# Cross attention's key and query units as products of 512 columns, with VectorE adding the halves

## What is computed

```python
def memory_attention(h, mem_n, w_q, w_kv, w_out):      # h: 256 x 1024, mem_n: 256 x 1024
    q = (h @ w_q).reshape(b, s, XA_HEADS, XA_HEAD_DIM)  # 4 heads of 256
    k, v = jnp.split(mem_n @ w_kv, 2, axis=-1)
    sc = jnp.einsum('bshd,bmhd->bhsm', q, k) * XA_HEAD_DIM ** -0.5
    p = jax.nn.softmax(sc, axis=-1)
    o = jnp.einsum('bhsm,bmhd->bshd', p, v).reshape(b, s, D_MODEL)
    return o @ w_out
```

## Time and profile before

| | |
|---|---|
| median of 3 runs | 1280.35 us (1280.28 to 1281.39) |
| the profiled execution | 1280.76 us, of which the trace's span is 1278.9 us |
| TensorE matmul busy | 1252.3 us, 98% of the span |
| VectorE, ScalarE, GpSimd busy | 929.4 us (73%), 680.6 us (53%), 77.9 us (6%) |
| mean granted TensorE clock | 0.998 of full speed |

### The profile page before, as it was taken

How to read it: one execution, slowest core, us unless ns; L and a number is a source line. 1 busy time by engine, 2 the same in 40 slices (tenths; PEclk the granted TensorE clock), 3 DMA queues, 4 the chain that set the end, 5 groups by cost and what they waited for, 6 DMA issues and landing times. The chain is left out here.

```text
span 1278.9 us, 18653 instructions
## 1 busy us (share of the span) xinstructions
PE 1252.3 (98%) x7688; PEld 1115.2 (87%) x7688; DVE 929.4 (73%) x1290; ACT 680.6 (53%) x868; POOL 77.9 (6%) x94
## 2 busy tenths in 40 slices
PE   7999999999999999999999999999999999999997
PEld 7878999989988888889998888888888988988886
DVE  5665857775456666575997997788888858788877
ACT  5555253443553444454776655466655564566652
POOL 2010000101000000000002331000000000000000
PEclk9999999999999999999999999999999999999999
DMA  8664555656535665546556654565554643655550
GB/s 284 209 184 132 166 164 166 219 192 199 180 99 164 197 187 182 192 137 197 177 185 205 202 189 149 198 198 195 181 186 134 204 154 108 213 183 188 198 194 37
DMA packets 159748, 227.98 MB, mean 178 GB/s; under 512 B 5517, under 2 KB 122001, under 8 KB 159536
## 3 DMA queue, kind: packets, MB, share of 16 engines
q1 hardware_dynamic: 156544, 216.68, 53.1%
q0 software_dynamic: 2816, 9.52, 2.3%
q10 hardware_dynamic: 304, 0.59, 0.1%
HBM read 225.68 MB, written 1.10 MB: 177 GB/s over the span
## 5 line engine op out<-in xcount | busy, mean ns | idle before, releaser
L1244 DVE TENSOR_TENSOR wlo<-raw,whi 128x2048 fp32r<-128x2048 f32 (+3 forms) x188 | 419.7, 2244 | 118.9 <-ACT whi L789 118.5
L789 ACT ACTIVATE whi<-raw 128x2048 fp32r<-128x2048 f32 (+2 forms) x187 | 348.0, 1874 | 19.8 <-DMA raw<-in_w_xkv 6.6
L2045 PE MATMUL psum<-h_both,whi 128*128 128x512 f32 x714 | 254.7, 396 | 0.0
L2013 PE MATMUL psum<-h_both,whi 128*128 128x256 f32 x704 | 200.6, 285 | 0.2 <-DVE wlo L1244 0.2
L2044 PE MATMUL psum<-h_both,wlo 128*128 128x256 f32 x714 | 199.4, 279 | 0.3 <-DVE h_both L1289 0.3
L2015 PE MATMUL psum<-h_both,wlo 128*128 128x256 f32 x704 | 199.1, 283 | 0.0
L2014 PE MATMUL psum<-h_both,whi 128*128 128x256 f32 x704 | 199.1, 283 | 0.0
L2013 PE MATMUL psum<-whi,r_hi 128*128 128x512 f32 (+1 forms) x464 | 181.0, 390 | 1.4 <-DVE arena L1588 0.7
L2015 PE MATMUL psum<-whi,r_lo 128*128 128x512 f32 (+1 forms) x464 | 178.1, 384 | 0.0
L2014 PE MATMUL psum<-wlo,r_hi 128*128 128x512 f32 (+1 forms) x464 | 178.0, 384 | 0.0
L2045 PEld LDWEIGHTS psum<-h_both,whi 128*128 128x128 f32 x714 | 134.0, 188 | 27.6
(11 more groups left out here) (331 smaller groups left out, 1858.2 us busy)
## 6 DMA issues: line engine op xcount, KB each, us to landing
raw<-in_ffn_up SPq DMA_DIRECT2D x44, 1024.0 KB, 5.1
raw<-in_w_in SPq DMA_DIRECT2D x32, 1024.0 KB, 5.8
raw<-in_ssd_in_proj SPq DMA_DIRECT2D x24, 1024.0 KB, 5.4
raw<-in_ffn_down SPq DMA_DIRECT2D x22, 1024.0 KB, 4.9
raw<-in_w_up SPq DMA_DIRECT2D x16, 1024.0 KB, 5.5
raw<-in_w_down SPq DMA_DIRECT2D x16, 1024.0 KB, 4.9
raw<-in_w_xkv SPq DMA_DIRECT2D x8, 1024.0 KB, 5.4
raw<-in_ssd_out_proj SPq DMA_DIRECT2D x8, 1024.0 KB, 5.0
```

Of the source, the lines that this page charges most:

```text
L789: A(whi[u % SLOTS][:, 0:kt * n], raw[u % SLOTS][:, 0:kt * n], ACT.Copy).then_inc(hi_split, 1)
L1244: V.tensor_tensor(wlo[s][:, 0:kt * n], raw[s][:, 0:kt * n], whi[s][:, 0:kt * n].bitcast(F32), ALU.subtract).then_inc(lo_split, 1)
L2013: M(o, a_hi, b_hi, start=start, stop=False)
L2045: return M(b[:, :], w_hi_k, h_both[:, :, k, :], start=False, stop=k == kt - 1)
```

## The change

Key and query units are made by `both_unit` instead of `b_unit`. Each gets two banks, 0 and 1 or 2 and 3 in turn. `r_hi` and `r_lo` become halves of one tensor `r_both`, so that the query's activations can be one moving operand. On ScalarE `copy_bank` becomes `low_copy`, and on VectorE `add_halves` is put in: for key unit j ahead of the j-th of the four splits behind `rms_out`, for query unit k at the end of head step k, behind the low part of a head's output. "Drained" of these keys is now signalled by VectorE.

```diff
     for j in range(4):
         p.unit(("xk", j), w["w_xkv"][0], 0, KD, 256 * j, 256)
-        p.gemm(("xk", j), ("xk", j))
+        for c in range(2):
+            p.gemm(("xk", j, c), ("xk", j), 2 * (j % 2) + c)
...
             p.unit(("xq", k), w["w_xq"][0], 0, KD, 256 * k, 256)
-            p.gemm(("xq", k), ("xq", k))
+            for c in range(2):
+                p.gemm(("xq", k, c), ("xq", k), 2 * (k % 2) + c)
...
-        r_hi, r_lo = sb("r_hi", [P, KD, T], F32R), sb("r_lo", [P, KD, T], F32R)
+        r_both = sb("r_both", [P, 2, KD, T], F32R)
+        r_hi, r_lo = r_both[:, 0], r_both[:, 1]
...
                 hi()
-                copy_bank(kT[:, 2 * j:2 * j + 2, :], ("xk", j), pair)
+                low_copy(kT[:, 2 * j:2 * j + 2, :], [("xk", j, c) for c in range(2)])
...
                     hi()
-                    copy_bank(qT[:, 2 * k:2 * k + 2, :], ("xq", k), pair)
+                    low_copy(qT[:, 2 * k:2 * k + 2, :], [("xq", k, c) for c in range(2)])
...
             rms_out(hN, xn, 0, 2)
-            for _ in range(4):
+            for j in range(4):
+                add_halves(kT[:, 2 * j:2 * j + 2, :], 0, [("xk", j, c) for c in range(2)])
                 lo()
...
                 if k >= 3:
                     part_bank(h_lo, h_hi, ("xo", k - 3), slice(2 * (k - 3), 2 * (k - 3) + 2))
+                if k < XA_HEADS:
+                    add_halves(qT[:, 2 * k:2 * k + 2, :], 0, [("xq", k, c) for c in range(2)])
                 if k >= XA_HEADS:
                     lo()
...
             for j in range(4):
-                b_unit(at[("xk", j)], h_hi, h_lo, one(("xk", j)))
+                both_unit(at[("xk", j)], [("xk", j, c) for c in range(2)])
...
                 if k < XA_HEADS:
-                    b_unit(at[("xq", k)], r_hi, r_lo, one(("xq", k)), ready=None if k else xT_ready("h2"))
+                    both_unit(at[("xq", k)], [("xq", k, c) for c in range(2)], x_both=r_both, ready=None if k else xT_ready("h2"))
                 if 1 <= k <= XA_HEADS:
                     i = k - 1
-                    wait_drained(pe, ("xk", i))
-                    wait_drained(pe, ("xq", i))
+                    for c in range(2):
+                        wait_drained(pe, ("xk", i, c))
+                        wait_drained(pe, ("xq", i, c))
```

More of the change, by code:

```diff
@@ L813, in copy_bank, with low_copy @@
                 A(dst, src(b), ACT.Copy).then_inc(drained[use[key][0]], 1)
+            def low_copy(dst, keys):
+                b0 = use[keys[0]][0]
+                for key in keys:
+                    wait_bank(act, key)
+                A(dst, psum[:, b0:b0 + 2, T:2 * T], ACT.Copy).then_inc(low_out, 1)
             def xT_parts(name, dst):
@@ L956, in _ @@
                 scaled_part_bank(h_hi[:, 2 * j:2 * j + 2, :], ("h3", j), G_MLP + 2 * j)
[L958 to L963, removed]
             def mlp_group(g):
@@ L2037, in b_unit, with both, both_unit @@
                 last.then_inc(unit_used, 1)
-            def both(b, w_hi_k, w_lo_k, k, kt):
+            def both(b, w_hi_k, w_lo_k, k, kt, x_both=h_both):
                 if k == 0:
[L2042 to L2047, removed]
+                    M(b[:, :], w_hi_k, x_both[:, :, k, :], start=True, stop=False)
+                    return M(b[:, 0:T], w_lo_k, x_both[:, 0, k, :], start=False, stop=False)
+                M(b[:, 0:T], w_lo_k, x_both[:, 0, k, :], start=False, stop=False)
+                return M(b[:, :], w_hi_k, x_both[:, :, k, :], start=False, stop=k == kt - 1)
+            def both_unit(u, keys, between=None, x_both=h_both, ready=None):
                 w_hi, w_lo, kt, _ = weights(u)
@@ L2054, in both_unit @@
                     for k in range(kt):
+                        if ready is not None and c == 0:
+                            ready(k)
                         cs = slice(P * c, P * c + P)
-                        last = both(b, w_hi[:, k, cs], w_lo[:, k, cs], k, kt)
+                        last = both(b, w_hi[:, k, cs], w_lo[:, k, cs], k, kt, x_both)
                 last.then_inc(unit_used, 1)
```

## The result

The changed kernel took 1288.02 us (median of 4 runs, 1287.65 to 1288.62), against 1280.32 for the kernel before beside it (4 runs): a ratio of 1.0055 [1.0043, 1.0068]. That is 7.7 us slower, where +3.77 was forecast and 1285.8 was the end of the range. The direction was right, the size was off by twice.

What follows compares the result with a forecast made beforehand. TensorE, busy 1252.3 of 1278.9 us, was taken to bound the kernel. The terms -1.36 + 2.45 + 0.05 + 2.63 = +3.77 us on a median of 1280.35 gave 1284.1 us, range 1282.6 to 1285.8.

Steps and rivals of the forecast that it cites:

- Part 1: All eight key and query units: wider products take 5.59 us a unit instead of 5.76, -1.36 us in all.
- Place A: Key unit 2 waits for the sums of key unit 0, behind VectorE's split and hN: +2.45 us.
- Place B: The value units wait for the sums of key unit 2: +0.05 us, ends 0 and 0.3.
- Place C: Scores 3 wait for the sums of query unit 3, behind head 0's low part on VectorE: +2.63 us.
- rival 4: Key and query units: wider products win little, units stay near 5.7 us; +4.8, 1285.1 us; chance 3%.
- Part 2: Evacuation: ScalarE's copy stays, VectorE gains 5.9 us of additions; three places can wait, elsewhere the additions are hidden.
- handoff: At the new waits: TensorE goes on 0.05 us after VectorE's addition ends.
- restart: After a wait, the first product holds the next back by 0.34 instead of 0.23 us.
- Rival 1: Only one of the two large waits binds: +1.1, 1281.5 us, within 0.2%; chance 8%.
- Rival 2: Time lost at the waits is made up at later TensorE waits: +0.3, 1280.6 us; chance 5%.
- rival 3: The clock falls to 1.2 GHz at the waits for one unit, 5.6 us each: 1289.7 or 1295.3 us; chance 4%.

Runs made afterwards that it cites:

- e12: The changed kernel measured once more, unedited: 1287.02 us, ratio 1.0042; its profiled execution is the run of 1285.23 us.
- e6: The kernel before, with one added wait: key unit 2 starts only when hN is written; 1283.36 us, ratio 1.0016.
- e1: The changed kernel with its query units put back as before, so only the key units are changed; 1284.18 us, ratio 1.0024.
- e3: The changed kernel with each query unit's sums moved ahead of the maximum of the scores in VectorE's order; 1284.52 us, ratio 1.0023.
- e2: The changed kernel with its key units put back as before, so only the query units are changed; 1283.88 us, ratio 1.0021.
- e7: The changed kernel with key unit 0's sums put between the two tiles of hN, shortening the wait at key unit 2; 1286.21 us, ratio 1.0035.
- e4: The changed kernel with key units 2 and 3 in banks 4 to 7; 1283.02 us, ratio 1.0015.
- e9: The changed kernel with nine unread matmuls of 512 columns into a free bank ahead of key unit 2; 1287.75 us, ratio 1.0051.
- e8: The kernel before, with one added wait: key unit 2 starts only when VectorE has split the first value unit; 1288.19 us, ratio 1.0056.
- e5: The changed kernel with the edits of both e3 and e4; 1279.71 us, ratio 0.9992.
- e10: The kernel before, with eight unread matmuls ahead of the transpose behind the second block's norm; 1280.33 us, ratio 0.9992.
- e11: e5 with eight unread matmuls ahead of the transpose behind the second block's norm; 1279.90 us, ratio 0.9991.

## Why the prediction was wrong in size

Against the execution without a fall (e12), step by step, shifts read as in the first section:

| step | forecast | measured |
|---|---|---|
| Part 1, eight units | -1.36 | -1.28 (5.59 us a unit in after; 0.16 each) |
| Place A, key unit 2 | +2.45 | +2.64 (-0.36 to +1.80 with three units at -0.16) |
| Place B, value units | +0.05 | +0.17 (value unit at 314.32 in after, 5.75 behind unit 3's start) |
| Place C, scores 3 | +2.63 | +2.83 (+1.20 to +4.03) |
| nothing | 0 | -0.36 at the start, +0.3 behind 367 us |
| sum | +3.77 | +4.3, inside the ends of +3.1 and +4.9 |

**Part 1** was right, and with it rival 4 was wrong: the rows of the MLP unit held for key and query units. **Part 2** was right: 16 additions more, VectorE 6.1 us busier (5.9 forecast), ScalarE's time unchanged, and no wait where the additions were called hidden. **Places A and C** were right in place and releaser, and each was 0.2 us too small. The term that was short is the handoff from VectorE's end to TensorE's start, which the prediction took from one pair of rows as 0.05 us and used for both: it measured 0.15 at key unit 2 and 0.25 to 0.28 at scores 3. (At key unit 2 the additions also began 13.14 us behind unit 0's start, where 13.07 was laid out.) The restart was right (301.32 to 301.63 in e12 is 0.31 us, against 0.23 in a stream). That the trace shows 2.35 and 2.56 us of idle time where 2.35 and 2.53 were forecast is luck: it counts from the modelled end of the last matmul, the forecast from the moment at which the next one could have started. Counted like the forecast the waits are 2.52 and 2.72. **Place B** was within its ends. **Rival 1** fell with both waits in every profile of the change. **Rival 2** fell with e6, where a shift of +1.95 us behind the wait was still +1.96 at 804 us.

**The step that failed: the sum has no term for the clock.** The prediction left it to rival 3, with 4% and the wrong size, because the longest pause inside the kernel, 2.2 us, had not moved the granted clock in the one profile of before. The row it read for that the earlier trace rows could not have shown a fall, as the page of after has two under the same row of nines. And that profile was taken for the rule, where it was one throw of several. Its paragraph on the chances even had the warning: three runs that differed by 1.1 us, which the prediction put down to an error of the medians. By their times they fit the two groups above: two runs without the fall (1280.28, 1280.35), and one (1281.39) with it. The count over the profiles, each of one execution:

```
pause ahead of                     idle us      clock fell in                       did not fall in
key unit 2                         2.35 to 2.4  after, e1, e3                       e12
scores 3                           2.56 to 2.6  e2, e7                              after, e4, e9, e12
transpose at the later norm        2.1 to 2.2   after, e1, e3, e6, e7, e8, e9       before, e2, e4, e5, e12
key unit 2, edited                 4.8          e8
key unit 2, edited                 1.7, 1.0, 0.31                                   e6, e7, e9
transpose at the norm, filled      0.34, 0.35                                       e10, e11
```

So the change adds two chances of a fall to the one that was there. In these thirteen falls the clock goes to half between 0.5 us before TensorE resumes (e7 at scores 3) and 1.3 us after (e3 at the norm). The eight runs of the change say how often the chances are taken: 1285.23 with none, one at 1286.23, and six from 1287.65 to 1288.62, which is where two falls or three would put them. The size was off the other way: not 5.6 us for a whole unit at half clock but 1.4 (key unit 2, after against e12), 1.4 (e2 at scores 3, a step of 4.25 against 2.83) and 1.1 (the norm, between the groups of before), since the clock is full again before the unit ends (in after it is at half from 301.2 to 304.6, the unit runs to 308.57).

The Trainium skill (TensorE: Matmul & The Clock Gate, section "Why this matters for your kernels") warns of idle gaps as sending the clock to half rate. The traces agree behind 4.8 us and, in some executions, behind gaps from 2.1 us on, shorter than the gaps that section names. The same page (section "What's actually happening") has the hardware's observation run free of the kernel; by that, one and the same gap could do it in one execution and not in the next. The runs fit this, but none shows what decides it, and that stays open.

**What the medians mix.** The forecast was made from a median of 1280.35 whose runs were mostly without a fall. Against the longer series of before, 1281.36, the change of e12 is +5.7 rather than +7.7. Both comparisons are of the kernels as they run; a part of either is how the falls happened to lie.

**A version without the waits.** e5 and e11 keep the wide units and give the sums a place where nobody waits: 1279.71 and 1279.90, against 1280.91 and 1281.36 of before beside them, so 1.2 and 1.5 us less, at the edge of what the intervals resolve (0.9984 to 1.0001, 0.9983 to 1.0000); that they are faster than before is likely, not shown. Against e10, which has the pause filled too, e11 gains 0.43 us, and its slowest run (1280.04) is faster than the fastest of e10 (1280.16): that is what the mended change is worth here, of 1.28 us won where the wide units stand. In the profile of e11 the shift is -1.71 us at 363 us and -1.27 at the end, of which -0.43 was there before the key units; some 0.4 us is lost again on the way, 0.35 of it behind the later norm (see the last section).

## What to carry to other kernels

When a result's evacuation moves to another engine, read that engine's program, not its load: VectorE was free a quarter of the time, and both waits came from what stood ahead of two short additions in its order; four more banks and one moved line took them away. A pause of the matmul engine of about 2 us may cost its length plus 1 to 1.5 us, and whether it does can differ from one execution to the next, so one profile without a fall proves nothing; runs that fall into two groups with different mean clocks are the sign to look for. A pause that can't be shortened can be filled with matmuls into a free bank; none of the 22 runs of e10 and e11 lies in an upper group.

## What was unexpected

A pause present in the kernel before was already deciding between two groups of its runs, 1.1 us apart, and eight matmuls whose output nobody reads took the upper group away (e10).

Behind the norm of the second block VectorE stands still for 0.3 us in all eight profiles of kernels with both halves of the change (after, e3, e4, e5, e7, e9, e11, e12), and in none of before, e1, e2, e6, e8 and e10. In e12, VectorE and then TensorE there:

```profile
811.77 0.69 DVE L1272 TENSOR_TENSOR h_both<-psum,h_both 128x512 fp32r<-128x512 f32 x1 [0.29 <-issue]
```

```profile
814.58 0.66 PE L2133 MATMUL psum<-cst,xn 128*128 128x128 f32 x4 [0.20 <-DVE xn L1407]
```

The shift of TensorE grows by 0.35 us there in e4, e5, e11 and e12, where the clock was full, and behind the fall of after by nothing more, which is why that fall is worth 0.8 us against e12. So this much of the change's cost is neither a wait for the sums nor the clock, and it is most of what e11 loses on the way. "issue" means that the profile shows nothing VectorE waited for; the cause stays open.

At 728 us, some 360 us behind the last changed instruction, the shift grew by 0.7 us. VectorE and GpSimd over time there, of before and then of after:

```profile
725.36 1.56 POOL L746 TENSOR_TENSOR arena<-arena,cst 128x256 f32<-128x256 f32 x1 [5.21 <-DMA arena<-decay_rows]
...
726.71 1.36 DVE L1761 TENSOR_TENSOR arena<-arena,row_d 128x512 f32<-128x512 f32 x2
```

```profile
732.51 1.84 DVE L1767 TENSOR_TENSOR arena<-arena,row_d 128x512 f32<-128x512 f32 x2
732.72 1.08 POOL L749 TENSOR_TENSOR arena<-arena,cst 128x256 f32<-128x256 f32 x1 [6.69 <-DMA arena<-decay_rows]
```

In after, GpSimd's operation waited longer for the transfer of a decay row (6.69 us against 5.21) and began beside this VectorE pair instead of 1.35 us ahead of it, and the pair took 1.84 us instead of 1.36. That the one comes from the other is read from these rows alone. From 700 to 740 us the shift grew by 0.1 to 0.4 us in e5, e7, e9, e11 and e12 too, and in e1 to e4 it moved by 0.1 at most. Why the transfer lands when it does was not tried either.
